# TensorE waits for its own last tile ahead of each group of four gate/up tiles and each pair of output tiles; one feed-forward's input rows are moved to another address

## What is computed

```python
def swiglu(x, w_gu, w_down):                     # first model, four times
    gate, up = jnp.split(x @ w_gu, 2, axis=-1)
    return (jax.nn.silu(gate) * up) @ w_down

def macaron_ffn(x, pre_g, post_g, w_gate, w_up, w_down):   # second model, four times
    h = swiglu_2(rms_norm_2(x, pre_g), w_gate, w_up, w_down)
    return x + MACARON_WEIGHT * rms_norm_2(h, post_g)
```

## Time and profile before

| | us |
|---|---|
| median of 3 runs | 2390.57 |
| lowest and highest | 2387.93, 2390.97 |
| the profiled execution, its own time | 2389.72 |
| its span, first to last instruction | 2387.9 |
| mean granted TensorE clock | 0.975 of full |
| PE busy in the span | 95% |

### The profile page before, as it was taken

One profiled execution on the slowest core, in us unless ns is written; L12 is line 12 of the kernel. 1 busy time (PEld: TensorE's weight loads), 2 busy tenths in 40 slices (PEclk: granted clock), 3 DMA queues, 4 the chain that ended last, 5 costly groups with the idle time before them and its releaser, 6 DMA issues.

```text
span 2387.9 us, 49098 instructions
## 1 busy us (share of the span) xinstructions
PE 2266.1 (95%) x18270; PEld 2226.8 (93%) x18270; DVE 1401.0 (59%) x1966; ACT 1161.6 (49%) x1752; POOL 555.8 (23%) x589
## 2 busy tenths in 40 slices
PE   7999999999999999999999999986999999978998
PEld 7999888999999999889999899976999999978998
DVE  6555856655555557666565565576653655365553
ACT  5544544454445446444554454466554455445553
POOL 4321000232223220002332232124430133112420
PEclk9999999999999999999999999998999999988999
DMA  6555423455546544233565366452664656533663
GB/s 214 184 184 163 133 89 119 141 172 175 178 149 192 190 157 154 90 98 121 173 192 201 124 199 197 140 162 81 196 206 144 202 183 199 166 104 108 186 193 112
DMA packets 99258, 380.47 MB, mean 159 GB/s; under 512 B 10911, under 2 KB 13087, under 8 KB 99016
## 3 DMA queue, kind: packets, MB, share of 16 engines
q1 hardware_dynamic: 99144, 378.91, 49.4%
HBM read 377.80 MB, written 3.16 MB: 160 GB/s over the span
## 4 chain that ended last, share of the span: by engine, by line
PE 83%; DVE 7%; ACT 4%; issue 3%; DVEq 2%; POOL 1%; POOLq 1%; DMA 0%; ACTq 0%; SPq 0%
PE bank L607 25%; PE bank L609 24%; PE bank L608 24%; DVE wlo L1394 2%; ACT whi L995 2%; PE bank L662 1%; PE bank L879 1%; PE bank L663 1%; PE bank L664 1%; PE bank L625 1%; POOLq L1955 1%; PE bank L789 1%; PE bank L868 0%; DVE cv L1730 0%; PE bank L858 0%
## 5 line engine op out<-in xcount | busy, mean ns | idle before, releaser
L1394 DVE TENSOR_TENSOR wlo<-raw,whi 128x1024 fp32r<-128x1024 f32 (+1 forms) x660 | 870.4, 1330 | 530.0 <-ACT whi L995 527.6
L995 ACT ACTIVATE whi<-raw 128x1024 fp32r<-128x1024 f32 (+1 forms) x660 | 728.9, 1117 | 453.5 <-PE bank L609 421.7
L607 PE MATMUL bank<-x_tokens_hi,wlo 128*128 128x256 f32 x1456 | 410.9, 282 | 4.4 <-DVE z L1746 3.9
L608 PE MATMUL bank<-x_tokens_lo,whi 128*128 128x256 f32 x1456 | 409.5, 281 | 0.0
L609 PE MATMUL bank<-x_tokens_hi,whi 128*128 128x256 f32 x1456 | 409.4, 281 | 0.0
L1975 POOL TENSOR_TENSOR z<-sil,z 128x256 f32<-128x256 f32 (+1 forms) x176 | 172.8, 982 | 576.9 <-DVE z L1438 428.8
L607 PEld LDWEIGHTS bank<-x_tokens_hi,wlo 128*128 128x128 f32 x1456 | 274.6, 189 | 4.9 <-issue 4.1
L608 PEld LDWEIGHTS bank<-x_tokens_lo,whi 128*128 128x128 f32 x1456 | 278.7, 191 | 0.0
L609 PEld LDWEIGHTS bank<-x_tokens_hi,whi 128*128 128x128 f32 x1456 | 276.0, 190 | 0.0
L607 PE MATMUL bank<-hid_tokens_hi,wlo 128*128 128x256 f32 x704 | 197.8, 281 | 0.0
L608 PE MATMUL bank<-hid_tokens_lo,whi 128*128 128x256 f32 x704 | 197.8, 281 | 0.0
(11 more groups left out here) (400 smaller groups left out, 5675.3 us busy)
## 6 DMA issues: line engine op xcount, KB each, us to landing
raw<-ffn_gu SPq DMA_DIRECT2D x352, 512.0 KB, 3.6
raw<-ffn_down SPq DMA_DIRECT2D x128, 704.0 KB, 4.1
raw<-mix SPq DMA_DIRECT2D x120, 512.0 KB, 3.5
raw<-rec SPq DMA_DIRECT2D x28, 512.0 KB, 4.1
raw<-kv SPq DMA_DIRECT2D x16, 512.0 KB, 4.5
raw<-att SPq DMA_DIRECT2D x16, 512.0 KB, 3.9
bias_rows<-rows SPq DMA_DIRECT2D x8, 256.0 KB, 4.2
bias<-bias_rows SPq DMA_DIRECT2D x1, 1536.0 KB, 9.1
```

The lines of the kernel that those rows point to most:

```text
L607: pe.matmul(out, wlo[:, slot, w], xh(i), start=(i == 0), stop=False)
L608: pe.matmul(out, whi[:, slot, w], xl(i), start=False, stop=False)
L995: act.activation(whi[:, k, 0:cols], raw[:, k, 0:cols], ACT.Copy).then_inc(hi_made, 1)
L1394: dve.tensor_tensor(wlo[:, k, 0:cols], raw[:, k, 0:cols], whi[:, k, 0:cols].bitcast(F32), ALU.subtract).then_inc(lo_made, 1)
```

## The change

Two waits are added on TensorE, on the counter that TensorE's own tiles count up. The first is at the head of each round of four gate/up tiles: `b * RING + j` is the number of all tiles before this round. The second is at the head of each pair of output tiles, again for all tiles before it. Apart from that F6 gets the input buffers that the other feed-forwards of the second model use.

```diff
-             "F5": x_tokens, "F6": pair_at("x_back", KD, xbase + BACK_SHIFT, SEQ), "ATT": x_tokens, "F7": x_tokens}
+             "F5": x_tokens, "F6": x_tokens, "ATT": x_tokens, "F7": x_tokens}
...
-               "F6": pair_at("hid_back", KF, hbase + BACK_SHIFT, SEQ), "F7": hid_tokens}
+               "F6": hid_tokens, "F7": hid_tokens}
...
                 with pe.Fori(2, FFN_GU_QUADS) as b:
+                    pe.wait_ge(tile_done, b * RING + j)
                     for k in range(RING):
                         k8_tile(b + q, k, b * RING + j + k - 3, k, X[s], c)
                 def down(b, last=False):
+                    pe.wait_ge(tile_done, b * 2 + j + 2 * KF)
                     for m in range(2):
```

## The result

| | before | after |
|---|---|---|
| median, us | 2389.25 (4 runs) | 2420.07 (4 runs) |
| lowest and highest | 2371.67, 2390.97 | 2419.74, 2421.52 |
| the profiled execution, its own time | 2389.72 | 2421.52 |
| its span | 2387.9 | 2419.7 |

The ratio is 1.0146, its 95% interval 1.0118 to 1.0175: the change makes the kernel 1.5% slower, 31 us. The prediction was 2416 us. Executions of the kernel before differ by up to 20 us among themselves, those of the kernel after by 1.8. The experiments show one cause of such differences; the execution at 2371.67 us was not profiled, so that it is this one's too is not shown.

A forecast was written before the change was run, and what follows sets the result against it. TensorE's matmul stream was taken as the bound. From the profiled 2389.7 us, waits add 58.4 (36.0 rounds, 22.4 pairs) and the faster pace gives back 31.5: 2416 us forecast, 8-in-10 range 2398 to 2452.

The forecast's parts named there:

- TensorE's stream is the bound; a stop is paid in full: Whole kernel: TensorE's matmul stream sets the time and nothing covers an added wait; 104 waits cost 58.4 us.
- 0.50 us per round: Head of each gate/up round: wait, wake, two register steps and slow second matmul; 72 rounds cost 36.0 us.
- The floor of 0.31: Each added wait: lower bound of its cost if register steps are free, 0.31 us, or 32.2 us in all.
- The upper bounds 0.57 and 0.85: Rounds and pairs: cost in us per wait if register steps are 0.03 slower, 68.2 us in all.
- 0.70 us per pair: Head of each output pair: a round's cost plus two more steps behind the wait; 32 pairs cost 22.4 us.
- Two paces, and a stop can change to the faster: 256-column feed-forwards: stable paces of 0.1133 and 0.1177 us per matmul; a fresh start may fall into the faster.
- all fast: Likeliest case: every 256-column matmul under the waits takes the faster pace; 2416 us, chance 0.42.
- all slow: Rival: drained starts in the 256-column loops fall into the slow pace, so nothing is gained; 2448 us, chance 0.23.
- mixed: Rival: some places start fast and some slow, giving half the gain; 2432 us, chance 0.20.
- The gain of 31.5 us: Five 256-column feed-forwards: 0.0044 us less on each of 6960 matmuls, 30.6 us, or 31.5 with F6's first 192.
- With 272 columns nothing: The 272-column feed-forwards: their 4176 matmuls gain nothing, since no start brings the pace of another level.
- F6's rows at 192 never 276: F6 on line 609 before the change: 279 ns at all 328 matmuls and never 276, read as the slower pace.

The follow-up runs named there:

- the two other kernels with the same waits on the same rows: The change with its waits only in the 256-column feed-forwards, 2397.03 us; the change with a wait ahead of every 272-column gate/up tile, 2457.66 us.
- the runs of one and two stops: Against the kernel after: one wait ahead of each 256-column gate/up loop, none inside, 2370.28 us; with a second ahead of the output pairs, 2371.68 us.
- the one-stop kernel: Against the kernel after: one wait ahead of each 256-column feed-forward's gate/up loop, none inside the loops, F6's rows at 64; median 2370.28 us, ratio 0.9932.

## Why the prediction was right, and where its terms were off

- *TensorE's stream is the bound; a stop is paid in full.* Right. The chain stays PE, and 27 more stops in a loop cost 27 times the same.
- *0.50 us per round.* 0.506 (0.524 + 0.218 - 0.236), but for F5, below. Its parts are shown too: 0.18 of it went when the wait moved behind the register steps, against 0.17 predicted. The floor of 0.31 was rounded down from 0.324, and the 0.32 measured is the unrounded one. The upper bounds 0.57 and 0.85 are too high for steps 0.03 slower: two and four of them give 0.56 and 0.82.
- *0.70 us per pair.* 0.68 with 256 columns and 0.69 with 272, in 28 of the 32. In the other four, the fourth pairs of F4 to F7, it is 0.32, since they are written out and have constants and no register steps. I had seen `down` as one case; the 1.5 us are a miss of reading the code, not of the chip.
- *Two paces, and a stop can change to the faster.* Right. *The forecast "all fast" against "all slow" or "mixed".* Nearly all fast in this execution: 43 of 45 rounds, 18 of 20 pairs. The four executions of this kernel agree within 1.8 us, so here the case is a steady one, and the two other kernels with the same waits on the same rows (43 and 45 of 45 rounds fast, 17 of 20 pairs in both) bear it out. But with F6's rows at 192, 10 of 45 rounds and 13 of 20 pairs were slow in the one execution, 2433.81 us, and the mixed rival stood at 2432. Nothing in the prediction's rows told the two cases apart: that the likeliest came, at a chance of 0.42, was in part luck.
- *The gain of 31.5 us.* Mis-sized by some 3: two slow rounds in `last` (11.91 and 11.86 us in place of 11.41), two slow pairs at the end of F6 (16.28 in place of 15.67, and 15.87 in place of 15.31), 2.1 together. And a fast round behind a stop needs 11.413 us where 0.1133 throughout would give 11.39, 45 times, about 1.
- *F5.* Not predicted at all. In eight of its nine rounds the first gap is 0.74 instead of 0.52:

```profile
1733.76 0.28 PE L609 MATMUL bank<-x_tokens_hi,whi 128*128 128x256 f32 x1
...
1734.51 0.19 PEld L607 LDWEIGHTS bank<-x_tokens_hi,wlo 128*128 128x128 f32 x1 [0.67 <-issue]
1734.52 0.38 PE L607 MATMUL bank<-x_tokens_hi,wlo 128*128 128x256 f32 x1 [0.48 <-PE bank L609]
```

  The last matmul starts at 1733.76 and the next weight load at 1734.51; the wait ends at 1734.08 as elsewhere, and the second register step at 1734.19 as well, but 0.21 us more pass before the weight load, with no semaphore late. It costs 1.7 us and comes back in the kernel with the waits alone. It is absent where the waits are left out with 272 columns (0.52 at each of F5's fast rounds; its loop is 1.42 us over before, 0.5 of it a slow round) and where they are put ahead of each tile there (all nine 0.52, 0.96 us over). Both edits change only code ahead of F5. That points to the place of the loop in the program; no run tested it, and the cause is open.
- *With 272 columns nothing.* Right for the sum (21.9 predicted, 23.0 measured), wrong as a statement. There are two paces there too: 123.4 and 126.7 ns per matmul. Rows at 64 mostly have the first, yet one output pair in each of the two `0` fell to 126.7 behind a stop. `x_second` at 192 has 126.7 in every round.
- *"F6's rows at 192 never 276".* As a reading of the trace right; as a reason wrong, since behind stops they had it. The move of the rows shows no difference in the program's times that can be told, but in the trace of the rows alone F6 is 6.0 us shorter, close to the 7 that the prediction gave as the most if its stream starts fast.
- *"A measurement can tell 5 us."* Too sure: it stood on three executions, and the fourth of the same kernel came 16 us below the lowest of them.

The sum then: predicted 26.9 over the profiled execution, measured 31.8. 272 columns +1.1; the written-out pairs -1.5; F5 +1.7; slow rounds and pairs +2.1; the slower approach to the pace +1; the rest are first gaps longer by 0.05 here and there, and what lies between.

The Trainium skill, "TensorE: Matmul & The Clock Gate", gives one formula for a single matmul ("Single matmul latency") and one for the gap in a stream ("Back-to-back issue gap"); their difference, 0.163 us per stop, was an estimate; the runs show 0.32 with the wait next to the matmul and 0.50 to 0.70 with register steps in front. That matmul's duration was right (276 ns against 272), but a stop costs more than the matmul's latency.

## What to carry over

A wait of TensorE on its own last tile costs 0.3 to 0.7 us of stream each, so one that recurs every 11 us must win more than 3 to 5% between two waits; one per 160 us costs 0.6 in 160. It isn't safe for all that: where the stream already had the faster pace, 3 of 7 such stops lost it, some 6 us each. If a stream of equal matmuls shows two paces at the same shape and clock, test one restart ahead of the long stretch, and take several runs, since the outcome is settled anew in each execution. Look first which stretches are slow ahead of the place. Put such a wait behind the register steps, next to the matmul: 0.18 us less per round and 0.36 per pair.

## What the runs showed of the chip that I had not expected

- Two stable paces for weight load and matmul at full granted clock: 113.3 and 117.8 ns with 256 columns, 123.4 and 126.7 with 272. A stretch without a stop keeps its pace, for some 1390 matmuls at least, and starts that agree to a few ns end in different ones (in the runs of one and two stops second gaps of 216, 217 and 222 ns came before the faster pace ahead of a loop, 217, 219 and 220 before the slower). By what the chip decides is open; the pace ahead of the stop alone does not.
- Spread between executions of one program on one core of 9 to 24 us at a granted clock of 0.973 to 0.979. Between two profiles of the one-stop kernel 18.5 of 21.9 us is the number of feed-forwards in the faster pace. The kernel with a stop ahead of each round and pair spreads by 1.8 us only.
- 0.09 to 0.11 us per register step on TensorE ahead of a matmul once it stands empty (the first to the second step of the round above 1427.79 to 1427.90), and 0.21 us in F5's rounds whose origin is open.
- No fall of the granted clock from 104 stops: 1.00 in every loop stretch, 0.977 over the span against 0.975 before.
